# Five tiles of 422 tokens instead of six of 352 in the projection stage of a fused hybrid layer

## The reference

```python
h = rmsnorm(x, norm_pre)
proj = jnp.einsum('bld,de->ble', h, w_in)          # all branches and gates at once
# A: gated linear attention: q, k, v, z columns, forget gates by a rank-16 projection
logf = jax.nn.log_sigmoid(gla_f @ gla_wf2 + gla_bf) / GLA_TAU
# B: causal pooling in windows 2, 4, 8, 16, a map per group, times SiLU(z)
# C: q, k, v through a causal convolution of width 4 and SiLU; q and k normalised:
q = l2norm(to_heads(cq, GDN_HEADS)) * (GDN_DK ** -0.5)
k = l2norm(to_heads(ck, GDN_HEADS))
# ... recurrences over chunks, output maps, sigmoid gates, w_out, rmsnorm, residual
```

## Time and profile before

| | |
|---|---|
| median of 3 executions | 2552.24 us (2550.89 to 2553.39) |
| profiled execution: its own time | 2555.57 us |
| profiled execution: span of the instructions | 2553.8 us |
| projection stage | 0 to 1143.5 us of the span |
| PE busy | 2476.2 us, 97% of the span |
| mean granted clock of PE | 0.981 |

### The profile page before, as it was taken

The page is one execution under the profiler, slowest core; times in us unless marked ns, Lnnn a source line. Parts: engine busy times, 40 slices in busy tenths (PEclk is TensorE's granted clock), DMA queues, the critical chain, the costliest instruction groups (busy, mean ns, idle before and its releaser), DMA issues. The chain is left out here.

```text
span 2553.8 us, 40027 instructions
## 1 busy us (share of the span) xinstructions
PE 2476.2 (97%) x15943; PEld 2384.8 (93%) x15943; DVE 1041.3 (41%) x1603; ACT 674.8 (26%) x1349; POOL 820.7 (32%) x711
## 2 busy tenths in 40 slices
PE   7999999999999999999999999999999979999998
PEld 7989999999999999998999999999999869999886
DVE  6620111134465662005554554545555443325332
ACT  6211111111255521113222332222332232223221
POOL 1211221121211212215545555445555213334222
PEclk9999999999999999999999999999999879999999
DMA  4213521111112122411432326432224345553543
GB/s 163 73 68 110 212 76 50 42 52 42 42 51 76 51 82 88 139 59 46 117 110 79 84 82 208 133 100 81 82 81 110 104 165 212 178 183 129 159 144 99
DMA packets 200200, 265.88 MB, mean 104 GB/s; under 512 B 16177, under 2 KB 175297, under 8 KB 194433
## 3 DMA queue, kind: packets, MB, share of 16 engines
q1 hardware_dynamic: 200064, 263.86, 32.1%
HBM read 164.54 MB, written 99.29 MB: 103 GB/s over the span
## 5 line engine op out<-in xcount | busy, mean ns | idle before, releaser
L178 POOL TENSOR_TENSOR w_hi<-w_raw,zero 128x1024 fp32r<-128x1024 f32 x77 | 148.3, 1926 | 1188.9 <-PE dense L348 824.8
L346 PE MATMUL dense<-h_hi_first,w_hi 128*128 128x352 f32 x1032 | 341.2, 331 | 0.7 <-POOL w_lo L180 0.7
L347 PE MATMUL dense<-h_lo_first,w_hi 128*128 128x352 f32 x1032 | 334.1, 324 | 0.0
L347 PE MATMUL dense<-h_lo_second,w_hi 128*128 128x352 f32 x1032 | 334.0, 324 | 0.0
L348 PE MATMUL dense<-h_hi_first,w_lo 128*128 128x352 f32 x1032 | 334.0, 324 | 0.0
L348 PE MATMUL dense<-h_hi_second,w_lo 128*128 128x352 f32 x1032 | 333.2, 323 | 0.0
L346 PE MATMUL dense<-h_hi_second,w_hi 128*128 128x352 f32 x1032 | 332.3, 322 | 0.0
L1360 PE MATMUL gate_bank<-h_hi_first,w_hi 128*128 128x352 f32 x768 | 275.7, 359 | 12.4 <-issue 5.1
L1360 PE MATMUL gate_bank<-h_hi_first,w_lo 128*128 128x352 f32 x768 | 250.4, 326 | 0.0
L1360 PE MATMUL gate_bank<-h_lo_first,w_hi 128*128 128x352 f32 x768 | 250.3, 326 | 0.0
L2205 PE MATMUL y<-o_hi,wo_hi 128*128 128x352 f32 x576 | 187.7, 326 | 14.2 <-DVE wo_lo L2249 12.8
(11 more groups left out here) (234 smaller groups left out, 4765.1 us busy)
## 6 DMA issues: line engine op xcount, KB each, us to landing
w_raw<-in_w_in SPq DMA_DIRECT2D x77, 512.0 KB, 5.8
rows_then_inputs<-scratch_feat SPq DMA_DIRECT2D x16, 1856.0 KB, 9.2
scratch_feat<-row_y SPq DMA_DIRECT2D x28, 1056.0 KB, 4.9
gate<-scratch_gates SPq DMA_DIRECT2D x12, 2112.0 KB, 8.5
scratch_gates<-gate_row SPq DMA_DIRECT2D x96, 176.0 KB, 2.3
o_raw<-scratch_branch_out SPq DMA_DIRECT2D x6, 2112.0 KB, 13.0
scratch_merged<-merged SPq DMA_DIRECT2D x48, 176.0 KB, 1.9
rows_then_inputs<-in_x_prompt SPq DMA_DIRECT2D x16, 512.0 KB, 3.6
```

Of the source, the lines that this page charges most:

```text
L178: nc.gpsimd.tensor_tensor(self.hi[:, p], raw, zeros, ALU.add).then_inc(self.high_ready, 1)
L346: nc.tensor.matmul(out, w_hi[:, p, k], h_hi[:, k, cols], start=(k == 0), stop=False)
L347: nc.tensor.matmul(out, w_hi[:, p, k], h_lo[:, k, cols], start=False, stop=False)
```

## The change

`PROJ_TILES` = 5 takes the place of `TILES` = 6 in the projection stage: tiles 0, 1, 3 and 4 have 422 tokens (two from each half), and tile 2 has 424, the last 212 tokens of the first half and the first 212 of the second. Its matmuls read them in one access pattern of two runs. For that the halves are addressed through one tensor `h` that spans both. As the number of tiles is odd now, the buffer of a tile is `(t + p) % 2` (and `(t + odd) % 2` in `sig` and `side`) so that buffers still alternate from block to block. The counts of all semaphores follow. In `conv_slot` the two conditions `t == 3` and `t == 4` stay as they are.

```diff
+PROJ_TILES = 5
+MIDDLE = PROJ_TILES // 2
+
+PROJ_W = 422
+MIDDLE_PART = HALF_TOKENS - MIDDLE * PROJ_W
+SIG_W = 2 * MIDDLE_PART
+
+def width(t):
+    return 2 * MIDDLE_PART if t == MIDDLE else PROJ_W
+
+class Halves:
...
+    def tile(self, k, t):
+        if t == MIDDLE:
+            at = self.starts[0] + k * HALF_TOKENS + MIDDLE * PROJ_W
+
+            step = self.starts[1] - self.starts[0] - MIDDLE * PROJ_W
+            return bass.AP(self.words[:, :].tensor, at, [[self.row, P], [step, 2], [1, MIDDLE_PART]])
+        half, start = (0, t * PROJ_W) if t < MIDDLE else (1, MIDDLE_PART + (t - MIDDLE - 1) * PROJ_W)
+        return self.halves[half][:, k, start:start + PROJ_W]
...
-    todo = [(t, f, k) for t in range(TILES) for f in range(2) for k in range(KD)]
+    todo = [(t, f, k) for t in range(PROJ_TILES) for f in range(2) for k in range(KD)]
...
-        while todo and len(now) < STEPS and j >= -(-(todo[0][0] + 1) * TW // P) - 1 + 2:
+        while todo and len(now) < STEPS and j >= -(-span(todo[0][0]).stop // P) - 1 + 2:
...
-                    pool.wait_ge(dense_ready, 2 * TILES - 1 + p)
+                    pool.wait_ge(dense_ready, 2 * PROJ_TILES - 1 + p)
...
-                    for t in range(TILES):
+                    for t in range(PROJ_TILES):
                         if ahead_of_tile is not None:
                             ahead_of_tile(t)
...
-                        h_hi, h_lo = hi[t // 3], lo[t // 3]
+
+                        out = dense[:, (t + p) % 2, 0:width(t)]
                         for k in range(KD):
-                            cols = slice(t % 3 * TW, (t % 3 + 1) * TW)
-                            out = dense[:, t % 2, 0:TW]
-                            nc.tensor.matmul(out, w_hi[:, p, k], h_hi[:, k, cols], start=(k == 0), stop=False)
-                            nc.tensor.matmul(out, w_hi[:, p, k], h_lo[:, k, cols], start=False, stop=False)
-                            mm = nc.tensor.matmul(out, w_lo[:, p, k], h_hi[:, k, cols], start=False,
+                            nc.tensor.matmul(out, w_hi[:, p, k], hi.tile(k, t), start=(k == 0), stop=False)
+                            nc.tensor.matmul(out, w_hi[:, p, k], lo.tile(k, t), start=False, stop=False)
+                            mm = nc.tensor.matmul(out, w_lo[:, p, k], hi.tile(k, t), start=False,
                                                   stop=(k == KD - 1))
...
-                        for t in (2 * tile, 2 * tile + 1):
+                        for t in range(2 * tile, min(2 * tile + 2, PROJ_TILES)):
...
-                    for t in range(TILES):
-                        if normed is not None and t < TILES // 2:
-                            norm_logs(j - 2, 2 * t)
-                            norm_logs(j - 2, 2 * t + 1)
-                        if normed is not None and t == TILES // 2 - 1:
+                    for t in range(PROJ_TILES):
+                        if normed is not None:
+                            for u in range(2 * t, min(2 * t + 2, PROJ_TILES)):
+                                norm_logs(j - 2, u, 1 - p)
+                        if normed is not None and 2 * t + 1 == PROJ_TILES:
                             norm_exp(j - 2, normed)
-                        act.wait_ge(dense_ready, j * TILES + (F_CONV * TILES + t + 1))
-                        write(t, dense[:, t % 2, 0:TW])
+                        act.wait_ge(dense_ready, j * PROJ_TILES + (F_CONV * PROJ_TILES + t + 1))
+                        write(t, dense[:, (t + p) % 2, 0:width(t)])
                         if t == 3 and not (isinstance(j, int) and j == 0):
```

More of the change, by code:

```diff
@@ L386, in opening_product @@
                             pe.wait_ge(act_free, 2 * t + f - 1)
[L387 to L392, removed]
+                    out = dense[:, f, 0:width(t)]
+                    nc.tensor.matmul(out, w_hi[:, f, k], hi.tile(k, t), start=(k == 0), stop=False)
+                    nc.tensor.matmul(out, w_hi[:, f, k], lo.tile(k, t), start=False, stop=False)
+                    mm = nc.tensor.matmul(out, w_lo[:, f, k], hi.tile(k, t), start=False, stop=(k == KD - 1))
                     if k == KD - 1:
@@ L422, in pool_map @@
                     pe.wait_ge(pool_d_ready, g + 1)
-                    for t in range(TILES):
-                        n = (2 + g) * TILES + t
+                    for t in range(PROJ_TILES):
+                        n = (2 + g) * PROJ_TILES + t
                         pe.wait_ge(side_free, n - 1)
-                        nc.tensor.matmul(side[:, n % 2, 0:TW], pool_w[:, g], X[:, 1, t * TW:(t + 1) * TW],
+                        nc.tensor.matmul(side[:, n % 2, 0:width(t)], pool_w[:, g], X[:, 1, span(t)],
                                          start=True, stop=True).then_inc(side_ready, 1)
@@ L671, in write @@
                     def write(t, tile):
-                        nc.scalar.copy(Y[:, p, t * TW:(t + 1) * TW], tile).then_inc(act_free, 1)
+                        nc.scalar.copy(Y[:, p, span(t)], tile).then_inc(act_free, 1)
                         if t == 2 and between is not None:
                             between()
-                    tiles(f, write)
+                    tiles(f, p, write)
                 def last_sigmoid():
@@ L1047, in _ @@
                 n = EARLY_GATES - 1
-                for t in range(0, TILES, 2):
-                    at = slice(t * TW, (t + 2) * TW)
-                    store(gates[:, n, at], Y[:, 0, at], act_free, (A_GATE + n) * TILES + t + 2, gate_stored[0])
+                for a, b in ((0, 1), (2, 3), (4, 4)):
+                    at = slice(span(a).start, span(b).stop)
+                    store(gates[:, n, at], Y[:, 0, at], act_free, (A_GATE + n) * PROJ_TILES + b + 1, gate_stored[0])
                 sp.wait_ge(caches_stored, 4 * 16)
@@ L2387, in program @@
             with ExitStack() as early:
-                hi_1, lo_1 = halves(early, ("h_hi_second", "h_lo_second"))
-                project_phase(nc, d, (hi_0, hi_1), (lo_0, lo_1), consts, weights, first)
-            chunk_phase(nc, d, consts, hi_0, lo_0, late, weights, first)
+                second_half = halves(early, ("h_hi_second", "h_lo_second"))
+                row = (second_half[1] - h_offset) // 4 + Halves.SIZE
+                words = nc.alloc_sbuf_tensor_at("h", [P, row], F32R, offset=h_offset)
+                hi, lo = (Halves(words, row, [(half[part] - h_offset) // 4 for half in (first_half, second_half)])
+                          for part in range(2))
+                project_phase(nc, d, hi, lo, consts, weights, first)
+            chunk_phase(nc, d, consts, hi[0], lo[0], late, weights, first)
         with nc.sbuf_tensor("late_bytes", [P, late.words], F32):
```

185 lines of the change are left out of this document (100 added, 85 removed).

## The result

| | before | after |
|---|---|---|
| median of 4 executions | 2552.81 us (2550.89 to 2554.39) | 2615.48 us (2613.16 to 2619.54) |
| ratio, with its 95% interval | | 1.0249 (1.0236 to 1.0262) |
| span of the profiled execution | 2553.8 us | 2613.5 us |
| mean granted clock of PE | 0.981 | 0.972 |
| last `dense` matmul of the projection stage starts | 1143.54 us | 1187.97 us (+44.4) |

The change costs 2.5%, where 1.0% was forecast; the time lies above the range. Of the 59.7 us of span, 44.4 are in the projection stage (forecast: 25) and 16.6 in the chunk stage (forecast: none).

A forecast was written before the change was run, and what follows sets the result against it. PE alone was taken to bound the projection stage, waiting repeatedly only at convolution block ends. Terms -14.9 + 25.3 + 13 + 2.5 - 0.6 - 0.3 = +25 us gave 2577 us, 1.0% slower; 8-in-10 range 2562 to 2587 us.

The forecast's parts named there:

- term 2: Convolution block ends in the projection stage: squares come later and PE waits for them, +25.3 us.
- term 3: PE's clock behind the stalls at convolution block ends: falls to 1.2 GHz after seven of them, +13 us.
- the clock holds through the stalls: Rival for the convolution block ends: no clock loss, the other terms alone, +12, 2564 us; chance 22%.
- term 4: Opening of the projection stage: first products start later and PE waits for scalings, +2.5 us (0 to 5).
- the split's wait: PE's wait at 84.75 for the split weights (0.65 us) goes, as the split has more cover: -0.6 us.
- Fewer, wider matmuls: Term 1, projection stage's `dense` matmuls: five wider tiles save part of a fixed 14.4 ns per matmul, -14.9 us.
- no start cost is saved: Rival for `dense` tiles: second run costs as much as a matmul start, +40, 2592 us; chance 6%.
- I take the second run at nothing: Middle tile of the projection stage: reading two runs costs nothing extra, bounded from above at +14.9 us.
- the small one that the forecast worked out: Term 1 by the Trainium skill's fixed part of about 2.5 ns per matmul: 2.6 us, making the sum +37.
- The chunk and closing stages only move: Stages after the projection stage: they only move in time, with no term in the sum.
- pool maps: Projection stage's pool maps have four ping-pongs with VectorE fewer in all: -0.3 us.

The follow-up runs named there:

- squares_early: Changed kernel with the sigmoid and squares of a convolution slot one tile sooner (`t == 2`, `t == 3`): 2571.94 us, ratio 1.0067 to the kernel before.
- five_peeled: Changed kernel with three of PE's last projection loop iterations written out ahead of the chunk loop, same work: 2604.4 us, ratio 1.0194 to the kernel before.
- middle_one_run: Changed kernel whose middle tile, from the third block on, reads one run of 424 tokens from the second half (other values): 2616.84 us, one execution.
- closing422: Kernel before with the closing stage's 512-column groups cut into 422 + 90 and 54 + 422 + 36: 2705.37 us, one execution, long through added narrow matmuls.
- closing480: Kernel before with the closing stage's 512-column groups cut into 480 + 32 and 448 + 64: 2643.86 us, one execution, long through added narrow matmuls.
- closing_shifted: Kernel before with the closing stage's first output half computed from `w_out` columns 54 to 565, so the moving operand starts 216 bytes on: 2559.58 us, one execution.
- six_squares_late: Kernel before, six tiles, with the sigmoid and squares one tile later (`t == 4`, `t == 5`): 2601.67 us, ratio 1.0192 to the kernel before.
- six_peeled: Kernel before with one iteration of PE's last projection loop written out ahead of the chunk loop, same work: 2556.33 us, ratio 1.001.

## Why the prediction was wrong

The sign and the mechanism that decides (the squares come late, PE stalls, the clock falls) were right; the size was not, through two steps.

**The stalls (term 2) were right.** Forecast +25.3 us; the eight block ends grew by 31.2 - 6.6 = 24.6 us. The chain of 8.31 us came out at 8.32 in the slot shown. Against PE's own pace of 0.19 us the sums came up to 3.87 us late (forecast 3.96), the first ones 2.73 (2.9).

**The clock (term 3) was right.** Forecast +13 us. The six low stretches hold 27.8 us of PE's busy time; at the 45% that the forecast lost in such a stretch that is 12.5 us, at half speed 13.9. Together with the stalls it is 37 to 39 us of the 44.4, and squares_early took 45 us away by removing both. The rival "the clock holds through the stalls" fell: it held through two of eight. The closeness of the figure is in part luck: with the same eight waits the low stretches hold 36 us of PE's busy time in five_peeled (all eight) and 19.5 us in middle_one_run (four), which at 45 to 50% is 16 to 18 us and 9 to 10 us. The six low stretches here are 3.3 us (twice) and 6.7 us (four times) long, which also differs between equal stalls; a single one could not be told.

**The opening (term 4) was right.** Forecast +2.5 - 0.6; the first product behind it starts at 87.06 against 84.75, +2.3 with the split's wait gone.

**The step that failed: "Fewer, wider matmuls".** It was to bring -14.9 us, from "what does not go by columns is 160.4 - 352 x 0.415 = 14.4 ns per matmul". That slope was drawn through one row of another stage, the 512 columns of the earlier trace rows. closing422, closing480 and closing_shifted show that this row is an exception: at other widths the closing stage takes 0.453 to 0.457 ns a column, and the same 512 columns take 234 ns once the moving operand starts elsewhere. Without it the seven widths of the table lie within 0.9 ns of one line with 0.447 ns a column and a fixed part of 3.8 ns in place of 14.4, and the step that was made, from 352 to 422 columns, costs 0.464 ns a column. The price of a row of tokens per product is 4 x 192.9 + 193.9 = 965.5 ns against 6 x 160.4 = 962.4 of six tiles: +3.1 ns x 24 x 43 = **+3.2 us** in place of -14.9, an error of 18 us. Thus the rival "no start cost is saved" came true in its effect (five tiles cost what six did) and not in its mechanism: it laid it on the second run, and middle_one_run puts that at 1.4 ns, 1.4 us in all. The forecast's "I take the second run at nothing" holds.

The Trainium skill ("TensorE: Matmul & The Clock Gate", section "Wait — 56ns, not 53.3ns?") has a warm start-to-start distance of columns / 2.4 GHz plus a fixed 2.5 ns. By it the gain of five tiles would be near the small one that the forecast worked out (2.6 us), and in this it was the better guide than my line. Its absolute distances are not those of these rows: an estimate from the page is 149 ns for 352 columns and 178 for 422, where this kernel's alternating weight loads and fp32r matmuls show 160.4 and 192.9.

**The other step that failed: "The chunk and closing stages only move".** The closing stage did (476.6 against 477.6). The chunk stage took 16.6 us more, with its work, shapes and order unchanged. squares_early shows that it isn't a late effect of the stalls (932.6), and six_squares_late the same from the other side (911.8); all kernels of five tiles whose loop is not written out have 930.2 to 935.8 us, whatever their width; writing out three iterations brings 920.8 and 916.9. So what the change did was to make PE's program ahead of the chunk loop shorter, and the loop's code came to lie elsewhere. The transfers of a queue that the profile names for instructions show what PE then waits for. First fence: that queue (packets, MB, share) over the whole chunk stage of the changed kernel; second fence: from 1310.9 to 1312.8 us, between the two stops shown above:

```profile
q8 instruction: 69, 1.13, 0.5%
```

```profile
q8 instruction: 1, 0.02, 5.9%
```

1.13 MB in 69 packets is 16 KB each. The kernel before, five_peeled and six_peeled also have 69 of them in this stage, so no more code is loaded. But the stops follow these packets closely. In the stops shown, a packet lands at 1308.80 and PE goes on at 1310.58; the next one moves from 1310.93 to 1312.71, and PE goes on from its second stop at 1314.05. Over the 17 traces all 102 first stops of an iteration end 1.70 to 1.92 us after a packet has landed, and the 42 second stops of the seven kernels of five tiles with the loop not written out, with the five of six_peeled, end 1.07 to 1.58 us after the landing of a later one. A distance this even over 149 stops says that PE stands because the code it needs is not there yet; no run changes the loading itself.

The place of the code then sets how much work covers the wait for that later packet. After the change PE has 7 matmuls between its two stops, in six_peeled 17. These 10 matmuls more, with a weight load each, are 20 instructions; by the counts of the expectation of five_peeled and six_peeled the loop lies 201 and 182 instructions into a piece, 19 apart. In the kernel before (116) and five_peeled (111) the end of the piece comes 85 to 90 instructions later than after the change, which I estimate at over 40 matmuls or 6 us more of cover, and there is no second stop.

The second stops make 12.2 us. PE's idle time as a whole rose by 11.1 us and its busy time by 5.4, with 71 us of this stage at the low clock where before it was 58.

**The sum as measured.** Stalls 24.6, clock 12.5 to 13.9, opening 2.3, tiles 3.2, pool maps -0.3 (the forecast's figure, not measured by itself): 42.3 to 43.7 us of the 44.4 in the projection stage. Ahead of the convolution two low stretches of the clock are 13.7 us long together and were 10.2, which can be the 1 to 2 us that are left; this length also differs between executions of the unchanged stage. Then 16.6 us in the chunk stage, -1 in the closing stage and -0.3 at the boundary: the span's 59.7 us.

**What stays open.** Why 512 columns at their own place in `w_out` come every 226.6 ns while the same width elsewhere takes 233 to 234: the start matters at this width, but the groups of 422 took 193.0 ns with and without a shifted start. Why five_peeled's chunk stage, with no second stop, is still 6.0 us above the 914.8 of before: its six first stops last 14.6 us together and were 11.6. Which of eight like stalls the clock falls behind.

## What to carry to other kernels

- Where a schedule is written by tile number (`t == 3`), a change in the number of tiles moves its steps in time. Work out what stands behind each such step before the tiles are costed: here two such numbers cost 37 to 39 us, and putting them one tile sooner was worth 5.4 us even without the change.
- The price of a matmul of a new width is not read off two points of which one lies in another stage. One more width measured in place would have shown that there was hardly a fixed part to save.
- "This stage only moves" is a claim too. Here a stage whose loop is fed with code as it runs changed by 1.8% when the program ahead of it got shorter. Hold it as a term of unknown sign, and before crediting an edit with a small gain, compare the stages that it did not touch; idle time at "issue" is set against the packets of the instruction queue.

## What was not expected of the hardware

- Distances of fp32r matmuls with a weight load each are close to proportional to the columns: 0.454 to 0.462 ns a column from 320 to 512, which leaves about 4 ns a matmul that fewer matmuls could save (the forecast had 14.4).
- At 512 columns the place of the moving operand is worth 7 ns of 227 (closing_shifted); at 422 a shifted start changed nothing.
- A moving operand in two runs costs 1.4 ns more a matmul at 422 to 424 columns and nothing visible at 512 (233.3 against 233.4).
- The chunk stage's 6615 matmuls take 912 to 936 us, depending on what code stands ahead of their loop. PE stops in each iteration until 1.7 to 1.9 us after a 16 KB packet of its code has landed, and where the end of the piece comes 7 matmuls later it stops again for 0.8 to 3.7 us.
- The same eight idle times of 2.6 to 3.7 us took PE's clock down six times in one execution (after), eight times in another (five_peeled) and four times in a third (middle_one_run).
